# Reordered modulation loads, a later shift, and 18 modulation tiles on TensorE, in a two-block transformer kernel on one core

## What is computed

```
silu_c = silu(c)
sh1, sc1, g1, sh2, sc2, g2 = split(silu_c @ w_mod + b_mod, 6)        # w_mod: 2048 x 12288
h  = rms_norm(x, g) * (1 + sc1) + sh1
y  = real(fft2(h in 8 groups of 256 columns, over rows and columns)) @ fnet_w_out
x  = x + g1 * rms_norm(y, ..)
x  = x + g2 * rms_norm(mlp(rms_norm(x, ..) * (1 + sc2) + sh2), ..)
```

## Time and profile before

| | |
|---|---|
| time, median of 3 runs | 2184.45 us (2181.9 to 2184.6) |
| span of the profiled execution | 2180.3 us |
| TensorE matmul busy | 2038.3 us (93%) |
| VectorE busy | 1270.9 us (58%) |
| ScalarE busy | 1020.5 us (47%) |
| read from HBM | 459.87 MB, 212 GB/s over the span |

### The profile page before, as it was taken

How to read it: one execution, slowest core, us unless ns; L and a number is a source line. 1 busy time by engine, 2 the same in 40 slices (tenths; PEclk the granted TensorE clock), 3 DMA queues, 4 the chain that set the end, 5 groups by cost and what they waited for, 6 DMA issues and landing times.

```text
span 2180.3 us, 24124 instructions
## 1 busy us (share of the span) xinstructions
PE 2038.3 (93%) x9141; PEld 1667.9 (76%) x9141; DVE 1270.9 (58%) x1191; ACT 1020.5 (47%) x1346; POOL 23.0 (1%) x25
## 2 busy tenths in 40 slices
PE   3499469999999999998999999999999999999997
PEld 1378358888888888887778778788888888888886
DVE  7978986555655454456546556654544454454454
ACT  3043245444444544444556654554445444544543
POOL 0000010000000000000000000000000000000000
PEclk9699669999999999999999999999999999999999
DMA  9999977666675555555454454455555555555552
GB/s 400 420 348 358 333 251 252 236 234 242 232 248 174 191 186 194 183 193 174 136 174 159 152 172 143 166 174 193 183 194 187 188 192 192 178 189 194 190 186 103
DMA packets 193757, 463.03 MB, mean 212 GB/s; under 512 B 7401, under 2 KB 7849, under 8 KB 180753
## 3 DMA queue, kind: packets, MB, share of 16 engines
q1 hardware_dynamic: 191808, 455.11, 60.6%
q0 software_dynamic: 848, 3.70, 0.5%
q10 hardware_dynamic: 1024, 3.20, 0.4%
HBM read 459.87 MB, written 2.10 MB: 212 GB/s over the span
## 4 chain that ended last, share of the span: by engine, by line
PE 86%; DVE 9%; ACT 2%; issue 1%; DMA 1%; ACTq 0%; DVEq 0%; SPq 0%
PE ps L419 27%; PE ps L421 27%; PE ps L420 27%; DVE scr L1107 6%; PE ps L455 2%; DVE w_low L1095 1%; DMA raw<-in_w_mod 1%; ACT w_high L779 1%; PE ps L555 0%; PE ps L557 0%; DVE h_both L1186 0%; PE ps L429 0%; PE ps L442 0%; PE ps L449 0%; ACT L993 0%
## 5 line engine op out<-in xcount | busy, mean ns | idle before, releaser
L1095 DVE TENSOR_TENSOR w_low<-raw,w_high 128x1024 fp32r<-128x1024 f32 x672 | 820.8, 1225 | 813.0 <-ACT w_high L779 812.8
L779 ACT ACTIVATE w_high<-raw 128x1024 fp32r<-128x1024 f32 x672 | 708.6, 1059 | 886.5 <-PE ps L421 870.1
L419 PE MATMUL ps<-w_high,h_both 128*128 128x512 f32 x1536 | 610.1, 397 | 8.5 <-DVE w_low L1095 7.6
L421 PE MATMUL ps<-w_high,h_both 128*128 128x512 f32 x1536 | 600.8, 391 | 0.0
L420 PE MATMUL ps<-w_low,h_both 128*128 128x512 f32 x1536 | 600.1, 391 | 0.0
L419 PE MATMUL ps<-w_high,u_high 128*128 128x512 f32 x1152 | 451.0, 392 | 0.3 <-DVE u_low L1489 0.3
L421 PE MATMUL ps<-w_high,u_low 128*128 128x512 f32 x1152 | 448.6, 389 | 0.0
L420 PE MATMUL ps<-w_low,u_high 128*128 128x512 f32 x1152 | 448.3, 389 | 0.0
L419 PEld LDWEIGHTS ps<-w_high,h_both 128*128 128x128 f32 x1536 | 289.8, 189 | 68.6 <-DVE w_low L1095 5.7
L421 PEld LDWEIGHTS ps<-w_high,h_both 128*128 128x128 f32 x1536 | 289.4, 188 | 62.0
L420 PEld LDWEIGHTS ps<-w_low,h_both 128*128 128x128 f32 x1536 | 290.0, 189 | 58.2 <-issue 0.5
(11 more groups left out here) (171 smaller groups left out, 819.9 us busy)
## 6 DMA issues: line engine op xcount, KB each, us to landing
raw<-in_w_mod SPq DMA_DIRECT2D x96, 1024.0 KB, 7.0
raw<-in_w_mlp_in SPq DMA_DIRECT2D x64, 1024.0 KB, 5.7
raw<-in_w_mlp_out SPq DMA_DIRECT2D x64, 1024.0 KB, 5.0
raw<-in_w_up SPq DMA_DIRECT2D x64, 1024.0 KB, 5.5
raw<-in_w_down SPq DMA_DIRECT2D x64, 1024.0 KB, 5.0
raw<-in_w_in SPq DMA_DIRECT2D x48, 1024.0 KB, 5.1
raw<-in_fnet_w SPq DMA_DIRECT2D x16, 1024.0 KB, 6.2
raw<-in_w_out SPq DMA_DIRECT2D x16, 1024.0 KB, 5.0
```

The lines of the kernel that those rows point to most:

```text
L419: eng.matmul(dst, ah, wh, start=(k == 0), stop=False)
L421: last = eng.matmul(dst, al, wh, start=False, stop=(k == KT - 1))
L779: eng.activation(w_high[:, h % LEAD, :], raw[:, slot, (h % 2) * 2 * CW:(h % 2 + 1) * 2 * CW], ACT.Copy).then_inc(high_ready, 1)
L1095: eng.tensor_tensor(w_low[:, h % LEAD, :], raw[:, slot, piece], w_high[:, h % LEAD, :].bitcast(f32), ALU.subtract).then_inc(raw_used if h ...
```

## The change

1. **Units renumbered and loads reordered.** Unit 0 is now scale 1 and unit 1 shift 1. The first 34 loads are the 16 tiles of scale 1 with the first five of shift 1 set among them (at loads 1, 3, 6, 10 and 14), the other 11 of shift 1, and two tiles of gate 1. Then come the 16 chunks of `fnet_w` with 1, 1, 2, 1 tiles behind them in turn (20 tiles), then what is left of shift 2 and scale 2. The total is still 96 loads.
2. **Shift 1 is added behind the channel DFT.** `turn_shift` transforms the shift with 8 small TensorE instructions, and `add_shift` adds it on VectorE to column 0 of `h_high` and `h_low`; the additions of L910 are gone. ScalarE's scaling waits for scale 1 alone. TensorE sums shift 1 just before the last DFT group.
3. **18 of the 80 tiles go to TensorE.** Tile by tile, TensorE multiplies the 16 pieces of 128x128 straight from the ring with one column of `silu_c` and accumulates in PSUM: five tiles of shift 1 (0 to 4), five of shift 2 (3, 5, 9, 12, 14) and eight of scale 2 (0, 2, 4, 6, 8, 10, 12, 15). Their slots are released by `raw_used_pe`. The column sums of the units add to the same PSUM columns. Scale 2's last tile is now the one on TensorE that is done by quarters.
4. **Small moves.** The first mean of squares comes after load 4, the row sum of gate 1 behind chunk 9 instead of 10, and the two halves of `scr` are swapped between units, so that GpSimd can clear gate 2's accumulator as soon as shift 2 is summed.

```
+EARLY_SHIFT = (1, 3, 6, 10, 14)
+BEHIND_CHUNK = (1, 1, 2, 1)
...
+ON_PE = sorted([AT[SH1, kk] for kk in range(len(EARLY_SHIFT))] + [AT[SH2, kk] for kk in (3, 5, 9, 12, 14)] +
+               [AT[SC2, kk] for kk in (0, 2, 4, 6, 8, 10, 12, 15)])
...
+            def mod_tile(unit, kk, bank):
+
+                n = AT[unit, kk]
+                eng.wait_ge(raw_loaded[n % RAW], 16 * (n // RAW + 1))
                 for j in range(KT):
...
+                    last = column_step(ps[:, at, j:j + 1], raw[:, n % RAW, j * P:(j + 1) * P],
+                                       silu_c[:, kk:kk + 1], first and j % (4 if unit == SC2 else KT) == 0, False)
+                last.then_inc(raw_used_pe, 1)
...
+            eng.wait_ge(silu_ready, 1)
+            for kk in range(3):
+                mod_tile(SH1, kk, 1)
...
+                if g in (1, 4):
+                    mod_tile(SH1, 3 if g == 1 else 4, 1)
+            last_read(SC1)
+            sum_partitions_to_columns(SC1, 3, False)
...
+                if g == FG - 1:
+                    last_read(SH1)
+                    sum_partitions_to_columns(SH1, 1, True)
...
+            turn_shift()
             eng.wait_ge(dft_low, FG)
+            eng.wait_ge(shift_added, 1)
...
                     if hh % 2 and ch == GATE_ROWS:
-                        sum_partitions_to_rows(2)
+                        last_read(G1)
+                        sum_partitions_to_rows(G1)
+                    if hh % 2 and ch in (12, 13):
+                        if ch == 12:
+                            eng.wait_ge(mod_cols, 3)
+                        mod_tile(SH2, 3 if ch == 12 else 5, SHIFT_BANK)
                 t.add("summed")
...
+            for kk in (9, 12, 14):
+                mod_tile(SH2, kk, SHIFT_BANK)
             eng.wait_ge(summed, NC)
-            sum_partitions_to_columns(3, 2)
-            norm_turn(0, 4)
+            mod_tile(SC2, 0, None)
+            last_read(SH2)
+            sum_partitions_to_columns(SH2, SHIFT_BANK, True)
+            for kk in (2, 4, 6):
+                mod_tile(SC2, kk, None)
+            norm_turn(0, 3)
+            mod_tile(SC2, 8, None)
             eng.wait_ge(mod_cols, 4)
-            t.add("raw", KT)
+            norm_turn(3, 4)
+            for kk in (10, 12):
+                mod_tile(SC2, kk, None)
             sum_scale_2_by_quarters()
```

More of the change, by code:

```diff
@@ L99, in add, with used @@
         self.c[name] += k
+    def used(self, d=0):
+        n = self.c["raw"] + d
+        return self.at("raw", d - sum(p < n for p in ON_PE))
     def arrived(self):
@@ L289, in mod_tile @@
             def mod_tile(unit, kk):
-                load(w_mod[bass.ds(kk * P, P), unit * D:(unit + 1) * D])
-            for i in range(RAW):
-                if i == 2:
+                column = MOD_COLUMNS[unit] * D
+                load(w_mod[bass.ds(kk * P, P), column:column + D])
+            for n, (unit, k) in enumerate(FRONT):
+                if n == 2:
                     eng.wait_ge(vec_in, 16 * 8)
[L296 to L314, removed]
+                if unit == FNET:
+                    chunk(fnet_w, k % 4 * 4 * P, k // 4 * CW)
+                else:
+                    mod_tile(unit, k)
             def mlp_chunk(w1, w2, q, ch):
@@ L409, in half @@
                     t.add("raw")
[L410 removed]
+                    eng.wait_ge(raw_used, t.used())
                 for tt in range(TT):
@@ L423, in half, with last_read @@
                 t.add("half")
-            def sum_partitions_to_columns(v, place):
-                if place:
-                    eng.wait_ge(mod_cols, t.c["mod_cols"])
-                for j in range(KT):
-                    last = eng.matmul(ps[:, 3, place * KT + j:place * KT + j + 1],
-                                      mod_acc(v)[:, j * P:(j + 1) * P], ones[:, 0:1], start=True, stop=True)
+            def last_read(unit, kk=KT - 1):
+                t.c["raw"] = AT[unit, kk] + 1
+                eng.wait_ge(raw_used, t.used())
@@ L434, in sum_scale_2_by_quarters @@
             def sum_scale_2_by_quarters():
+                last_read(SC2, KT - 2)
+                n = AT[SC2, KT - 1]
+                eng.wait_ge(raw_loaded[n % RAW], 16 * (n // RAW + 1))
                 for part in range(4):
[L437 to L443, removed]
+                    columns = range(4 * part, 4 * part + 4)
+                    for j in columns:
+                        last = column_step(ps[:, SCALE_BANKS[part], j:j + 1], raw[:, n % RAW, j * P:(j + 1) * P],
+                                           silu_c[:, KT - 1:KT], False, False)
+                    if part == 3:
+                        last.then_inc(raw_used_pe, 1)
+                    for j in columns:
+                        last = column_step(ps[:, SCALE_BANKS[part], j:j + 1], mod_acc(SC2)[:, j * P:(j + 1) * P],
+                                           ones[:, 0:1], False, True)
@@ L1284, in _ @@
[L1284 to L1295 removed]
+                if n == AT[SH1, KT - 1] + 1:
+                    mod_columns(SH1, 1)
@@ L1296, in _, with mod_behind @@
+            add_shift()
+            def mod_behind(ch):
+                for n in range(AT[FNET, ch] + 1, AT[FNET, ch + 1] if ch < 4 * NC - 1 else AT[SH2, 6]):
+                    front_tile(n)
+            for ch in range(4 * NC):
+                t.c["raw"] = AT[FNET, ch]
+                low_part()
+                low_part()
+                if ch == GATE_ROWS + 4:
+                    gate(1)
+                if ch >= 5 and ch % 4 == 1:
                     t.add("done", 8)
-                    add_step(None, c, c)
```

269 lines of the change are left out of this document (139 added, 130 removed).

## The result

The changed kernel takes 2231.55 us (median of 4 runs, 2229.34 to 2236.53) against 2183.61 for the kernel before in the same comparison (4 runs, 2181.9 to 2184.6). The ratio is 1.0218, 95% interval 1.0203 to 1.0233: slower by 48 us, where 29 were forecast, and 3.5 us above the upper end of the range. The profiled execution has a span of 2227.5 us, 47.2 more than before. One execution of the kernel before (3040 us) and one of the version with eight dense products in each tile (2280.6 us) ran in a slower state of the chip and stay out of all comparisons.

The account below looks back on a forecast made before the run. The front was taken as bound by VectorE's modulation tiles and nearly full DMA, with TensorE idle there. Terms -14.2 + 16.3 + 33.5 - 6.4 = +29.2 us gave span 2209.5, time 2213.7, range 2199 to 2228.

Parts of the forecast that it names:

- Step A: Up to the first chunk on TensorE: it comes at 128.3 us instead of 142.5, a change of -14.2.
- Step B: Chunk stage, first to last chunk: TensorE now waits for loads, length 108.7 us against 92.4, +16.3.
- t+16.5: End of gate 1's row sum in the chunk stage; t is chunk 9's landing, put at about 180 us.
- Rival 4: Chunk stage worse: waiting on a shift 2 tile drops the clock between chunks 12 and 15; 2219 to 2228 us, chance 0.15.
- Step C: Last chunk to scale 2's last column sum: 13 units in a row, twelve cold at 7.0 us; 94 against 60.5, +33.5.
- its twin: A column sum, same 32 instructions as a TensorE tile, used to price it: 3.63 us warm, 7.0 cold.
- Rival 1: Tail after the chunks: unbroken column products hold the clock, twelve units cost 3.63 us each; time 2177, chance 0.07.
- Step D: Last column sum to the flowing MLP: flows after 8.2 us, bounds 8 and 13, instead of 14.6; change -6.4.
- The mark of before: Start of flowing dense MLP matmuls in the kernel before, counted as a warm start at 310.1 us.
- rival 3: Chunk stage not bound by loads, as more are ahead: it ends at 226, time 2203 us, chance 0.14.

Follow-up runs that it names:

- the two versions whose last chunk came earlier: Changed kernel with shift 2 tiles 3 and 5 back on VectorE, with the row sum also behind chunk 10 (2216.10 us) or still behind chunk 9 (2222.58 us).
- the first experiment: Changed kernel with all 80 tiles on VectorE, keeping the new load order and the later addition of shift 1: 2190.60 us, ratio 1.0030 to the kernel before.
- the version without its waits in the chunk stage: Changed kernel with the row sum of gate 1 behind chunk 10 and shift 2 tiles 3 and 5 on VectorE: 2216.10 us, 1.0149.
- the last versions: Changed kernel, row sum behind chunk 10, shift 1 summed behind the last DFT group; four, no or two tiles on TensorE: 2182.16, 2182.41, 2181.27 us.

## Why the prediction was right in direction and wrong in size

**Step A** came out within 2.1 us, -12.1 for -14.2, and in part by luck, since errors inside it offset each other. The first three tiles cost 7.0 us as priced. VectorE had the last tile of scale 1 at 79.4, 3.9 us later than counted, but the sum behind it took 4.5 us instead of 7.0, with dense work up to 78.1 before it. The sum of shift 1 was warm as forecast, but the last DFT group behind it was half cold: 5.2 us from 119.35 on, where 3.43 were counted. The experiments split the whole. The order and the later shift bring the first chunk forward by 22.7 us, and the five tiles on TensorE take 10.6 of that back.

**Step B is the step that failed**, a term of the right sign and the wrong size: 120.7 us from the first to the last chunk where 108.7 were forecast (92.4 before), so 12 of the 18 us by which the forecast of the span was off. The sentence was "Row sum to t+16.5. From there TensorE is behind the loads: six chunks 32.7, two tiles of shift 2 warm 7.3", with 0.5 for the clock. Up to the end of chunk 9 the count of loads held (58.9 us for 59.7). Then, from the rows above: the wait for the gate's last tile was 6.3 for 5; the row sum, cold, 6.1 for 3.5; and from there to the end 49.4 for 40.5. Of those 8.9, 2.6 are the wait for the tile of load 66, 2.1 come from tiles that took 9.4 together for 7.3, and the other 4.2 are chunks at half clock, beyond the 0.5 that was counted for it: from 227.12 to 235.15 one chunk takes 8.0 us where 24 warm matmuls take 5.4, and the two chunks behind the warm tile take 12.6 where 48 warm matmuls take 10.9. So 3.63 us was the right price of a warm tile and not its whole cost: the clock falls while or just after it runs, and the dense work behind it pays another 1.7 us. The forecast had seen this in its own rows (the clock fell 3.5 and 4.6 us behind the last dense matmul) and did not apply it to the 5 us wait that it had itself worked out, nor to the chunks behind its warm tiles. Rival 4 had the right mechanism, but began it at the tile instead of the row sum, and its 2219 to 2228 us lie below the measured time too.

The waits feed each other. While TensorE waited for the gate and summed its rows cold, no half of a chunk was freed; ScalarE, which may be only four halves ahead, waited 8.25 us for it, the ring stood, and the DMA share was 0.55 from 202 to 217. These loads were missing at the tile behind chunk 12, whose wait let the clock fall again. This chain is read from the trace; no run moves the row sum alone while both tiles stay. Without both tiles the kernel gained 9 us, with the row sum moved back another 6. The last chunk came 19.7 us sooner by both, which is the 12 us by which this step was off and the 7.3 that the forecast had itself given to the tiles; some 5 of them are lost again in the tail.

**Step C** came out right: 93.1 us for 94, +32.6 for +33.5. The clock fell within the second tile (by the 0.82 of the window from 250 to 260, an estimate of 256.4, 5 us behind the last chunk). Each unit from the third on was cold and took 6.7 to 7.0 us, as its twin did. The waits for loads came to 5.3 us, some 2.5 more than the forecast had for them, and the first two tiles were 1.6 us and the other eleven units together 1.8 us quicker than counted. That the length met the forecast so closely is partly luck: with the same 13 units it was 98.3 and 102.9 us in the two versions whose last chunk came earlier. Nor are the +32.6 all the price of the tiles. Without any tile on TensorE this stretch takes 81.3 us in the new order (228.0 to 309.3, the first experiment), 20.8 more than before, since 27 loads instead of 21 lie behind the last chunk in the ring; the tiles add 11.8 to that. The forecast compared with the 60.5 us of the old order only. Rival 1, the clock held by an unbroken stream of column products, is refuted: TensorE was 93% busy for 70 us at 0.50, and busy without a wait for 34 of them. The Trainium skill (TensorE: Matmul & The Clock Gate, Why this matters for your kernels) names a continuously busy TensorE as what gives the full clock; this trace disagrees for column products, with a clock of 0.50 over that window. Adding dense products bears out that the kind of work counts. With eight in each tile the clock held for most of the time, but a tile then takes eight times 0.88 for four column instructions and a dense product, 7.0 us: what the clock gives is what holding it costs. With four it did not hold.

**Step D** was wrong by 5 us, at the far end of its own bounds: -1.6 for -6.4, worked out as the rest of the span. The cast beside GpSimd's clearing was on the path again, as the upper bound had it:

```profile
348.75 3.10 DVE L1267 CAST h_both<-extra 128x512 fp32r<-128x512 f32 x1
```

TensorE then waited 2.63 us for VectorE and went on warm at 353.76, 9.5 us behind the last column sum where 8.2 were forecast. So this cast explains only 1.3 of the 4.8 us. Behind it, two short waits for VectorE make the next 24 matmuls 1.1 us longer than warm ones without a gap (353.76 to 360.30), and between 450 and 550 us TensorE waits 1.6 us for VectorE's addition (L1278), a wait that the trace before doesn't have; the forecast had put everything behind the start of the MLP at no change. For the last 0.8 us no place was found. The mark of before was also set 0.4 us too late (310.1): the matmuls from 308.38 on were at half clock for 2.7 us only and lost 1.3.

**The accounts.** From the experiments: order and shift +7.4 (of which the place of the row sum 3.9), early tiles +9, the two tiles among the chunks +9, and the eleven in the tail what is left, some +23. That is 48. By another way, the version without its waits in the chunk stage less the one without tiles and with the row sum behind chunk 10 (32.9 - 3.5) less the early tiles leaves 20 for the eleven; no run has them alone. Against rival 3 speaks the DMA wait of ScalarE, 39.8 us. Why an earlier first chunk is worth so little by itself is answered by the last versions: it came 25 to 27 us earlier than before, and the last column sum 1 to 3 us later. The 80 tiles and 16 chunks pass one ring, and in the tail VectorE is busy 72 of 80 us with a DMA share of 0.97 to 1.00. The lead gained at the first chunk is lost as fewer tiles are done ahead of it. That these versions are still no slower than the kernel before lies behind that sum: without tiles on TensorE, the second half of the first MLP chunk starts warm 9.6 us behind it (307.23), before it started cold 12.9 us behind it (308.38). GpSimd clears gate 2's accumulator at 250.61 there, and at 295.55 before, where the casts of the MLP's start stood beside it; no run isolates this move. What stays open is how much of the tail is VectorE and how much the loads, since both are nearly full.

## What to carry to other kernels

A matrix-vector product on TensorE is priced by its weight loads and by the clock it finds, and it brings the low clock with it: take the cold price wherever it doesn't follow dense work at once, and charge the dense work behind it for the warm-up. When work moves from a full engine to an idle one, count how long it holds the shared buffer: slots held three times as long slowed the loads for both engines, and in the tail SyncE's queue waited 71.4 us for them. And when a forecast finds a wait of several microseconds on TensorE (5 or 6 us here), take what follows as cold until dense work has run; the buffers that it fails to free come back as the next wait.

## What was unexpected of the hardware

The clock fell in the middle of unbroken work more than once: in the second tile behind the chunks; 0.6 us into a dense chunk, behind a tile of 3.5 us; with four 128x256 products mixed into each tile 8.3 us behind the last chunk, while TensorE was full; and with eight in each tile, after holding from 246 us on, 1.7 us behind a wait of 1.18 us. There the mixture that had held the clock did not lift it from 298.8 to 309.2. It came back at 312.5, after 12 transposes of 128x128 in a row (309.23) and one more dense product; in the changed kernel 12 such transposes at 305.18 with column products behind them did not lift it. From 320 to 350 us the same mixture ran at 1.00 again. What exactly lifts it stays open. And holding it was no bargain: a column instruction with its weight load takes 0.113 us at 2.4 GHz and 0.214 at 1.2 (13.67 us for 64 of them in the tail), a dense product of 128x256 in two instructions 0.51 and 1.00.
